# The order of the NSA mix: odd units' copies inside the exponentials, a pair's parts at the start of its step, own scores before the compressed branch

## The reference, cut to what matters

```python
s_c = einsum(q, kc) * scale - slopes * dist_c         # compressed keys: 31 of them
p_c = softmax(where(valid_c, s_c, NEG_INF)); o_c = einsum(p_c, vc)
s_s = einsum(q, k_sel) * scale - slopes * dist_s      # selected blocks: with 8 blocks and top-16, all of them
o_s = einsum(softmax(where(mask_s, s_s, NEG_INF)), v_sel)
s_w = einsum(q, kw) * scale - slopes * dist           # window of 512
o_w = einsum(softmax(where(mask_w, s_w, NEG_INF)), vw)
return (gb[0] * o_c + gb[1] * o_s + gb[2] * o_w) @ w_out
```

## Time and profile before

| | |
|---|---|
| median of 3 runs | 2441.68 us (2439.95 to 2442.52) |
| span of the profiled execution | 2434.8 us (its own time is not given beside it) |
| PE busy over the span | 2345.5 us, 96% |
| DVE, ACT, POOL busy | 50%, 36%, 20% |
| this stage, first scores to the first product of the projection | 907.09 to 1071.55 us |
| PE busy in a period of eight units | 33.74 of 38.51 us |

### The profile page before, as it was taken

How to read it: one execution, slowest core, us unless ns; L and a number is a source line. 1 busy time by engine, 2 the same in 40 slices (tenths; PEclk the granted TensorE clock), 3 DMA queues, 4 the chain that set the end, 5 groups by cost and what they waited for, 6 DMA issues and landing times.

```text
span 2434.8 us, 27756 instructions
## 1 busy us (share of the span) xinstructions
PE 2345.5 (96%) x11055; PEld 1907.2 (78%) x11055; DVE 1205.3 (50%) x1869; ACT 877.5 (36%) x1359; POOL 482.4 (20%) x531
## 2 busy tenths in 40 slices
PE   6999889999999998889999999999999999999999
PEld 5888877888887766667888888888888767888887
DVE  4645846555424435645455434544334984444423
ACT  3322144554323336744333234223223453333221
POOL 0101732554102017730000010000010671000000
PEclk9999999999999999999999999999999989999999
DMA  7565005666323320002333323333232212333322
GB/s 252 177 195 182 1 29 162 189 187 194 117 91 106 91 73 1 1 19 86 95 95 93 98 96 95 97 102 97 96 109 88 81 35 70 95 96 96 103 95 78
DMA packets 169896, 247.43 MB, mean 102 GB/s; under 512 B 14890, under 2 KB 111335, under 8 KB 169767
## 3 DMA queue, kind: packets, MB, share of 16 engines
q1 hardware_dynamic: 155392, 198.70, 26.1%
q0 software_dynamic: 12464, 44.21, 5.9%
q10 hardware_dynamic: 1910, 2.74, 0.3%
HBM read 243.51 MB, written 2.10 MB: 101 GB/s over the span
## 4 chain that ended last, share of the span: by engine, by line
PE 85%; DVE 7%; ACT 4%; POOL 2%; issue 2%; DMA 1%; ACTq 0%; DVEq 0%; POOLq 0%
PE ps L562 75%; PE ps L1002 1%; ACT nsa_p L1629 1%; DVE w_lo L1858 1%; POOL hg_k L2657 1%; DVE dsa_mask L2423 1%; PE ps L534 1%; DVE small L2421 1%; PE ps L986 1%; PE ps L696 1%; DVE h_lo L1949 1%; ACT w_hi L1285 1%; DVE nsa_p L2319 0%; DMA vec_rows<-in_ffn_conv_b 0%; PE ps L1210 0%
## 5 line engine op out<-in xcount | busy, mean ns | idle before, releaser
L1858 DVE TENSOR_TENSOR w_lo<-w_raw,w_hi 128x1024 fp32r<-128x1024 f32 (+2 forms) x358 | 443.5, 1239 | 1017.0 <-ACT w_hi L1285 1016.7
L1285 ACT ACTIVATE w_hi<-w_raw 128x1024 fp32r<-128x1024 f32 (+2 forms) x364 | 380.5, 1046 | 1098.9 <-PE ps L562 1096.5
L562 PE MATMUL ps<-h_hi,w_hi 128*128 128x512 f32 (+1 forms) x1928 | 757.6, 393 | 8.6 <-DVE w_lo L1858 4.1
L562 PE MATMUL ps<-h_hi,w_lo 128*128 128x512 f32 (+1 forms) x1928 | 751.1, 390 | 0.0
L562 PE MATMUL ps<-h_lo,w_hi 128*128 128x512 f32 (+1 forms) x1928 | 750.9, 389 | 0.0
L562 PEld LDWEIGHTS ps<-h_hi,w_hi 128*128 128x128 f32 (+1 forms) x1928 | 361.7, 188 | 97.6 <-issue 11.1
L562 PEld LDWEIGHTS ps<-h_hi,w_lo 128*128 128x128 f32 (+1 forms) x1928 | 361.7, 188 | 76.4
L562 PEld LDWEIGHTS ps<-h_lo,w_hi 128*128 128x128 f32 (+1 forms) x1928 | 361.9, 188 | 76.1 <-issue 1.7
L562 PE MATMUL ps<-hid_hi,w_hi 128*128 128x512 f32 x704 | 275.5, 391 | 0.0
L562 PE MATMUL ps<-hid_hi,w_lo 128*128 128x512 f32 x704 | 274.0, 389 | 0.0
L562 PE MATMUL ps<-hid_lo,w_hi 128*128 128x512 f32 x704 | 273.9, 389 | 0.0
(11 more groups left out here) (380 smaller groups left out, 2471.3 us busy)
## 6 DMA issues: line engine op xcount, KB each, us to landing
w_raw<-in_ffn_w_up SPq DMA_DIRECT2D x264, 256.0 KB, 3.1
w_raw<-in_ffn_w_down SPq DMA_DIRECT2D x176, 256.0 KB, 2.8
m_raw<-in_ada_w POOLq DMA_DIRECT2D x80, 512.0 KB, 4.4
w_raw<-in_ffn_w_gate SPq DMA_DIRECT2D x88, 256.0 KB, 2.8
w_raw<-in_hg_w_in SPq DMA_DIRECT2D x64, 256.0 KB, 3.1
w_raw<-in_nsa_w_in SPq DMA_DIRECT2D x40, 256.0 KB, 2.9
w_raw<-in_w_in SPq DMA_DIRECT2D x32, 256.0 KB, 2.8
m_acc<-in_ada_w SPq DMA_DIRECT2D x9, 512.0 KB, 5.1
```

What stands on the lines that cost most here:

```text
L562: ins = K.nc.tensor.matmul(out, lhsT, rhs, start=start, stop=stop)
L1285: K.nc.scalar.activation(K.half(K.w_hi[u % SPL], width), K.half(K.w_raw[u % RAW], width), ACT.Copy) \
L1858: K.nc.vector.tensor_tensor(K.half(K.w_lo[u % SPL], width), K.half(K.w_raw[u % RAW], width), hi, ALU.subtract) \
```

## The change

Four moves in the order of the three engines' programs; no instruction is added, removed or altered.

1. ScalarE copies the turned weights of odd units one step earlier, in step u+2 instead of u+3, between the second and the third exponential of that step. Even units' copies stay at the start of step u+3. Even steps have no copies any more.
2. ScalarE's `high` and VectorE's `low` stand at the start of their step, ahead of the copies, not at its end.
3. TensorE does the unit's own scores first. On even steps `compressed` follows them, on odd steps it ends the step, behind `turn`.
4. ScalarE's compressed part 5 (the copy of the turned compressed weights) stands between the second and third exponential of its step, not ahead of the first.

```diff
 # tensor_nsa_mix
-        if 1 <= n < UNITS:
-            compressed((n - 1) // 8, (n - 1) % 8)
         if n < UNITS:
             for slot in range(3):
                 scores(n, slot)
+        if n % 2 == 0 and 1 <= n < UNITS:
+            compressed((n - 1) // 8, (n - 1) % 8)
...
         if 0 <= n - 2 < UNITS:
             for bank in (4, 5, 6):
                 turn(n - 2, bank)
+        if n % 2 and n < UNITS:
+            compressed((n - 1) // 8, (n - 1) % 8)
 # scalar_nsa_mix
+    def keep(u):
+        keep_turned(u, 4)
+        keep_turned(u, 6)
+
     for n in range(UNITS + 4):
-        if 0 <= n - 3 < UNITS:
-            keep_turned(n - 3, 4)
-            keep_turned(n - 3, 6)
-        if 1 <= n < UNITS and (n - 1) % 8 == 5:
-            compressed((n - 1) // 8, 5)
+        if n >= 7 and n % 4 == 3:
+            high((n - 7) // 4)
+        if n % 2 and 0 <= n - 3 < UNITS:
+            keep(n - 3)
         if n == 0:
             gates()
         if n < UNITS:
-            for t in (3, 2, 0, 1):
+            for t in (3, 2):
+                weights(n, t)
+        if n % 2 and 0 <= n - 2 < UNITS:
+            keep(n - 2)
+        if 1 <= n < UNITS and (n - 1) % 8 == 5:
+            compressed((n - 1) // 8, 5)
+        if n < UNITS:
+            for t in (0, 1):
                 weights(n, t)
...
-        if n >= 7 and n % 4 == 3:
-            high((n - 7) // 4)
 # vector_nsa_mix
     for n in range(UNITS + 4):
+        if n >= 7 and n % 4 == 3:
+            low((n - 7) // 4)
         if 0 <= n - 3 < UNITS:
             keep_turned(n - 3)
...
-        if n >= 7 and n % 4 == 3:
-            low((n - 7) // 4)
```

## The result

The changed kernel takes 2416.73 us (median of 4 runs, 2415.82 to 2418.72) against 2440.81 for the kernel before beside it: a ratio of 0.9902, 95% interval 0.989 to 0.9914, some 24 us faster. The prediction said 2420.2, range 2417.5 to 2429. Two later sets of runs gave 0.9901 (0.9882 to 0.9921) and 0.9893 (0.9874 to 0.9913). Two single executions of the kernel before, of 3328.77 and 4762.24 us, are slow ones that stand far outside all others and enter no figure here.

A forecast was written before the change was run, and what follows sets the result against it. No engine bounds the mix by its work; waits between engines do. Gains of 6.5 (start), 13.6 (periods) and 1.35 (end) sum to 21.45, taking 2441.68 to 2420.2 us; range 2417.5 to 2429.

The forecast's parts named there:

- The steady part: Three periods of eight units in the mix: 14.2 us of idle PE less 0.6 of waiting for POOL, 13.6 gained.
- All four stops: PE's idle times in a period: 1.14, 1.66 and 0.29 us before value products, 1.70 before compressed transposes; all go.
- POOL at T(19): PE's transposes of unit 19 wait 0.3 us for POOL, in the two periods where POOL makes the next bias.
- The coupling of copy and split: An even pair's value products wait for ACT's copies and DVE's low part, ending together; moving only one gains nothing.
- The compressed branch: ACT copies the compressed scores while PE does the next unit's scores; the 1.70 us stop before the compressed transposes goes.
- The start: First units of the mix: POOL takes c_p 6.5 us earlier, passed on whole; 5.5 if the products run at 1.2 GHz.
- The end: Last units of the mix: final value products start 1.4 us earlier, PE's first projection product comes 1.35 us earlier.
- The copies between exponentials: On ACT, 64 copies cost what they did, without table reloads; a reload at each would put 41 us on ACT.
- (a): Rival: value products' stops stay, only the compressed branch's part works; 2430.1 us, or 2424 to 2429 in between; chance 0.15.
- (b): Rival: POOL sets the pace, every odd unit's scaling delaying PE by 0.5 us; 2428 us; chance 0.12.
- (c): Rival: waits only traded, late odd transposes holding ACT, the reciprocal and the next scaling; gain under 4.9 us; chance 0.07.
- (d): Rival: slower, DVE stands at the reciprocal with later reductions and scores behind it; 2446 us, about 2447 by reloads; chance 0.04.

The follow-up runs named there:

- copy_third: Changed kernel with odd units' copies behind the third exponential instead of the second; 2419.26 us, ratio 0.9912 to the kernel before.
- copy_late: Changed kernel with odd units' copies back at the start of the next step, high and low still first; 2422.75 us, ratio 0.9928 to the kernel before.
- split_late: Changed kernel with high and low back at the end of their step; 2438.32 us, ratio 0.9994 to the kernel before.
- again_after: Changed kernel run once more without an edit; 2412.69 us, ratio 0.9901 to the kernel before.
- third_after: Changed kernel run a third time without an edit; 2413.03 us, ratio 0.9893 to the kernel before.
- pe_order: Kernel before with only TensorE's order changed, ScalarE and VectorE as before; 2427.05 us, ratio 0.9955 to the kernel before.
- bias_gap: Changed kernel with POOL making groups 1 to 3's compressed bias behind its scaling in steps numbered 1 of eight; 2412.54 us, ratio 0.9893 to the kernel before.

## Why the prediction was right and where it was wrong

**The steady part**: right. 13.6 foretold; 38.50 + 38.51 + 38.35 less 33.88 + 33.85 + 33.31 is 14.3. All four stops went, and what took their place is the one named, POOL at T(19), 0.3 foretold and 0.34 and 0.31 measured, absent in the last period. The extra 0.7 is a size that the prediction had wrong: a stop costs more than its bracket. Without one, PE's rows start 0.07 to 0.16 ahead of the modelled end of the row before, and with it they can't; the last period, with the same products and no stop, lasts 33.31. So the floor was 33.3, not 33.7: the four stops of 4.79 cost 38.51 - 33.31 = 5.20, and POOL's single stop of 0.34 or 0.31 costs 0.57 or 0.54. The weak spot was the slack before the values. It was said to be 0.2 to 0.4 and was about 0.03. The first copy did end 3.40 behind T(12) as foretold (981.03 + 0.58 is 981.61, against 978.20), but PE's row stood at 3.57, not 3.64, and where the values wait for this copy (copy_third, copy_late) they start 0.14 behind its end. That the stop went whole was luck.

**The coupling of copy and split**: right, and shown by both halves. Copies alone (split_late) leave nothing of the gain, and the stops, now 1.88 and 2.41, are longer than the 1.14 and 1.66 before, since the split then stands behind the copies; the split alone (copy_late) leaves stops of 0.77 and 1.30. That both "end together" was off by 0.25: the low part came last, as shown under the result.

**The compressed branch**: right. Its stop went with TensorE's order, and the start's 2.8 twice with it.

**The start**: 6.5 is what happens when PE keeps the high clock: 6.6 in again_after (1.00), where POOL takes c_p 13.30 behind the first scores against 19.94 before, 6.64 earlier. It was 6.4 in third_after (0.89 in that window) and 4.8 in the first trace (0.85). The sentence that failed is "at 1.2 GHz ... 5.5": it took only the compressed products as slow, and S(1) and the small products before them were slow too. The reason given for the high clock, that only idle times of 2.8 were followed by low pace, was too strong. In the first trace the clock fell within S(0), 1 us behind the end of a stop of 1.72: its product of 256 columns at 911.53 took 0.50 where the same one of S(2) takes 0.33; in split_late the pace fell behind stops of 1.88 and 2.41, and in pe_order behind one of 2.40. The page "TensorE: Matmul & The Clock Gate" of the Trainium skill (Part 1: The HAM clock gate) says that the moment of such a change depends on where the chip's free-running observation stands when the work begins. The three starts of one kernel (33.61, 31.77, 32.01) agree with that; they don't prove it.

**The end**: 1.35 foretold, 1.24 measured.

**The copies between exponentials**: free. ACT's groups by line over the mix show 64 copies of 478 ns, as many and as long as before, and one table load in front of the exponentials:

```profile
L1639 ACT ACTIVATE nsa_pT<-ps 128x512 f32<-128x512 f32 x64 | 28.6, 478 | 3.3 <-PE ps L986 3.0
...
L1631 ACT ACT_TABLE_LOAD x1 | 1.3, 1283 | 0.0
```

The 41 us that a reload at each would have put on ACT were not there. The page "ScalarE: Activation LUTs" of the Trainium skill (Table sets: the hidden batching unit) says that copy is in every set. This trace agrees with that.

**Rivals**: (a) the values' stops did not stay; (b) POOL sets the pace at one transpose of eight only, for 0.3; (c) and (d) did not come: the reciprocal stands 0.80, inside its slack of 2.5.

**The step that failed** is the last one, from the sum to the time. The sum for the mix, 21.45, against 20.35 in the first pair of traces and 164.9 - 143.0 = 21.9 as means of three each, was good. But "around it lie 6.9 us to the median, taken as unchanged" was false. Behind the change the median lies 2416.73 - 2415.8 = 0.9 above the traced span. The span itself came out 2.45 longer than the 2413.35 foretold, the median 3.5 shorter than the 2420.2. What lies around a span is 1.3; the other 5.6 were the difference between one execution, whose own time by that was 2436.1, and the median. The before median had come down by 0.9 when it was taken beside the changed kernel, so the median gained 24.1, 2.6 more than the sum: what the prediction put at nothing outside the mix was worth that much.

The executions show where it went. The kernel before took from 2429.9 to 2446.3 (mean 2439.2, standard deviation 3.4, over 76 runs of the later sets), the changed one from 2409.9 to 2421.4 (mean 2414.7, 3.4, over 16). Time goes with the mean granted clock: before's runs at 0.985 average 2444.5, those at 0.992 average 2434.1. One slope and one step fitted to all 92, an estimate, give 1.54 us for 0.001 of the clock and, at equal clock, 20.5 us between the kernels (standard error 0.4). The other 4.1 of the 24.6 go with the clock, on average 0.9918 for the changed kernel and 0.9891 for the one before. The low end of the range, 2417.5, lay 2.7 below the forecast, less than this scatter, since it was built from the costs of the work alone.

**Left open**: why the changed kernel's executions have the higher clock. A part of it lies in the start of the mix (window clocks 0.85, 1.00 and 0.89 against 0.91, 0.83 and 0.87). The mix with its low stretches explains 21.9 of the 24.6 (standard error of the difference 0.9); the other 2.7 lie outside it. No instruction differs there, and the difference is not in every pair of traces; whether the changed kernel, reaching the later stages 22 us sooner, meets the low clock less often there, or this is chance, these runs don't tell.

## What to carry to other kernels

When an instruction waits for two engines that finish within a few tenths of a microsecond, the one named in the chain may not be the one that ended the wait: list every semaphore that it waits for, compare the ends of their rows with its start, and move all, or nothing is gained. Read a slack from start to start of rows, and price a stop by the period without it (here 0.57 for a bracket of 0.34). Put an engine's independent products ahead of a short chain between engines, since each round trip is then covered by work; and after that look at what the slowest engine carries in the middle of its longest unbroken run, as bias_gap did for another 3.4 us of the mix. Add the scatter between executions to a range that was worked out from one trace, and compare kernels at equal granted clock where that scatter follows the clock.

## What the runs showed of the hardware

The clock of the same 34 us stretch of the same kernel was 0.85 in one execution and 1.00 in another, worth 1.8 us, with no different instruction ahead of it. The same stop ahead of the same sixteen value products, at the end of the mix, was followed by the high pace in the kernel before (2.41 us at 1065.88, products 2.38) and by the low one in pe_order:

```profile
1053.03 3.76 PE L1002 MATMUL ps<-nsa_pT,nsa_v 128*64 128x512 f32 x16 [2.40 <-ACT nsa_pT L1639]
```

Outside such stretches this schedule is exact: a period of 229 or 230 recorded products, waits on four engines included, repeats within 0.05 us over three executions of the changed kernel and within 0.11 over three of the one before.
